# Moving the last two latent query tiles behind the first maxima of the sliding-window attention

## The reference, cut to what matters

```
h = rms_norm(x, attn_norm[l]);  proj = h @ w_in[l]        # q, k, v, u, c_q, c_kv, k_rope
out_a = swa_mixer(q, k, v, ...)    # sliding window of 128, 6 heads of 64, 2 key heads, bias, sinks
out_b = pool_mixer(u, ...)         # windowed means of 2, 4, 8, 16 tokens, then a small product
out_c = mla_mixer(c_q, c_kv, k_rope, ...)   # latent attention, 6 heads of 64 + 32 rotary
x = x + concat(out_a, out_b, out_c) @ w_out[l]
x = x + (silu(h2 @ w_gate) * (h2 @ w_up)) @ w_down
```

## Time and profile before

| | |
|---|---|
| median of 3 runs | 2482.35 us (2479.43 to 2487.03) |
| the profiled execution | 2481.47 us |
| its span in the trace | 2479.7 us |
| mean granted TensorE clock | 0.974 |
| TensorE busy | 2331.0 us (94%) |
| GpSimd busy | 1661.9 us (67%) |
| VectorE busy | 1051.8 us (42%) |
| ScalarE busy | 501.6 us (20%) |
| DMA | 207.93 MB, mean 84 GB/s |

### The profile page before, as it was taken

How to read it: one execution, slowest core, us unless ns; L and a number is a source line. 1 busy time by engine, 2 the same in 40 slices (tenths; PEclk the granted TensorE clock), 3 DMA queues, 4 the chain that set the end, 5 groups by cost and what they waited for, 6 DMA issues and landing times.

```text
span 2479.7 us, 29722 instructions
## 1 busy us (share of the span) xinstructions
PE 2331.0 (94%) x11040; PEld 1901.3 (77%) x11040; DVE 1051.8 (42%) x1342; ACT 501.6 (20%) x955; POOL 1661.9 (67%) x1370
## 2 busy tenths in 40 slices
PE   5968999999996899999999699999999898999999
PEld 4766788888876678888887468888888776888887
DVE  7664533322366344332237545215334333540430
ACT  3245211110134521111012521001111263100000
POOL 5466677767756667777777577767766564776774
PEclk9988999999998899999999899999999999999999
DMA  4300122222330012222232112222232200222222
GB/s 145 107 27 18 68 102 95 91 87 93 117 107 18 18 69 102 97 89 87 94 124 102 52 68 88 99 102 96 91 119 86 86 35 17 85 102 102 85 102 85
DMA packets 37844, 207.93 MB, mean 84 GB/s; under 512 B 3532, under 2 KB 10316, under 8 KB 16888
## 3 DMA queue, kind: packets, MB, share of 16 engines
q1 hardware_dynamic: 37752, 206.70, 23.9%
HBM read 204.55 MB, written 2.13 MB: 83 GB/s over the span
## 4 chain that ended last, share of the span: by engine, by line
PE 60%; DVE 2%; POOL 2%; ACT 2%; issue 1%; DVEq 0%; POOLq 0%; ACTq 0%
PE ps L821 18%; PE ps L826 18%; PE ps L825 18%; POOL wl L649 1%; PE ps L1185 1%; PE ps L1159 1%; ACT rt L1335 1%; POOL wh L643 0%; PE ps L1160 0%; PE ps L1163 0%; PE ps L1161 0%; DVE sq L1705 0%; DVE t L1713 0%; DVE nt L1705 0%; PE ps L1200 0%
## 5 line engine op out<-in xcount | busy, mean ns | idle before, releaser
L649 POOL TENSOR_TENSOR wl<-raw,wh 128x512 fp32r<-128x512 f32 (+1 forms) x776 | 1032.8, 1361 | 0.0
L643 POOL TENSOR_SCALAR wh<-raw 128x1024 fp32r<-128x1024 f32 (+1 forms) x388 | 427.3, 1121 | 595.3 <-PE ps L821 462.6
L821 PE MATMUL ps<-h,wh 128*128 128x512 f32 x1576 | 618.1, 392 | 18.4 <-POOL wl L649 9.2
L825 PE MATMUL ps<-h,wh 128*128 128x512 f32 x1576 | 615.2, 390 | 0.0
L826 PE MATMUL ps<-h,wl 128*128 128x512 f32 x1576 | 615.1, 390 | 0.0
L821 PE MATMUL ps<-act,wh 128*128 128x512 f32 x1120 | 437.6, 391 | 1.1 <-DVE x L1705 1.1
L825 PE MATMUL ps<-act,wh 128*128 128x512 f32 x1120 | 436.0, 389 | 0.0
L826 PE MATMUL ps<-act,wl 128*128 128x512 f32 x1120 | 436.0, 389 | 0.0
L821 PEld LDWEIGHTS ps<-h,wh 128*128 128x128 f32 x1576 | 297.0, 188 | 85.5 <-issue 24.4
L825 PEld LDWEIGHTS ps<-h,wh 128*128 128x128 f32 x1576 | 296.9, 188 | 62.3 <-issue 1.0
L826 PEld LDWEIGHTS ps<-h,wl 128*128 128x128 f32 x1576 | 297.0, 188 | 62.1
(11 more groups left out here) (337 smaller groups left out, 2681.8 us busy)
## 6 DMA issues: line engine op xcount, KB each, us to landing
raw<-w_gu SPq DMA_DIRECT2D x44, 1024.0 KB, 4.8
raw<-w_up SPq DMA_DIRECT2D x32, 1024.0 KB, 4.8
raw<-w_down_b SPq DMA_DIRECT2D x32, 1024.0 KB, 4.8
raw<-w_down_a SPq DMA_DIRECT2D x32, 704.0 KB, 4.0
raw<-w_in_a SPq DMA_DIRECT2D x14, 1024.0 KB, 4.9
raw<-w_in_f SPq DMA_DIRECT2D x13, 1024.0 KB, 4.8
raw<-w_in_r SPq DMA_DIRECT2D x11, 1024.0 KB, 4.8
raw<-w_out_a SPq DMA_DIRECT2D x8, 1024.0 KB, 7.6
```

What stands on the lines that cost most here:

```text
L643: pool.tensor_scalar(hi_s[:, part], raw[s][:, part], 1.0, 1.0, ALU.mult, ALU.mult).then_inc(hi_done, 1)
L649: ins = pool.tensor_tensor(lo_s[:, part], raw[s][:, part], hi_s[:, part].bitcast(F32), ALU.subtract)
L821: first = pe.matmul(out, w_hi, v_hi, start=start, stop=False)
L825: pe.matmul(out, w_hi, v_lo, start=False, stop=False)
```

## The change

VectorE's loop over the six query tiles is cut to four, and its body becomes a function of its own. The last two tiles are taken in `attention`, behind `maxima(0, 1)` and ahead of `head_stat`. The counts are corrected by what `bk.close` and `sqr.n += 17` have added by then. The lists of the other engines are as before, and VectorE issues the same instructions as before in another order.

```diff
-                s0 = sqr.n
                 if l == 0:
                     dve.wait_ge(st_ext, 32)
-                for i in range(MLA_HEADS):
-                    b, u = (18 + i) % 4, (18 + i) // 4
-                    dve.wait_ge(ready[b], bk.filled(b, u))
-                    dve.wait_ge(sq_ready, s0 + 12 + i)
-                    tt(qc[0:96, i, :], ps[b][0:96, :], cgq[0:96, :], ALU.mult)
-                    tt(ts[64:96, :], ps[b][96:P, :], cgq[96:P, :], ALU.mult, bk.empties(b, u))
-                    tt(qc[64:96, i, :], qc[64:96, i, :], ts[64:96, :], ALU.add)
+                for i in range(4):
+                    latent_query(i, 0)
                 sqr.n += 17
                 bk.close(late(USES_IN_A))
+
+            def latent_query(i, closed):
+                b, u = (18 + i) % 4, (18 + i) // 4
+                u -= closed and late(USES_IN_A)[b]
+                dve.wait_ge(ready[b], bk.filled(b, u))
+                dve.wait_ge(sq_ready, sqr.n + (i - 5 if closed else i + 12))
+                tt(qc[0:96, i, :], ps[b][0:96, :], cgq[0:96, :], ALU.mult)
+                tt(ts[64:96, :], ps[b][96:P, :], cgq[96:P, :], ALU.mult, bk.empties(b, u))
+                tt(qc[64:96, i, :], qc[64:96, i, :], ts[64:96, :], ALU.add)
...
                 prep(m, l, 1)
                 maxima(0, 1)
                 if m.name == "swa":
+                    for i in (4, 5):
+                        latent_query(i, 1)
 
                     head_stat(5, -1, T, 1)
```

## The result

The changed kernel takes 2486.97 us against 2481.89 us before (medians of 22 runs each, taken in turn on one chip). The ratio is 1.0015 with a 95% interval of 1.0009 to 1.0021: 0.15% slower (2.2 to 5.2 us by the interval; the two medians are 5.1 us apart), where 2.8 us of gain were forecast, and above the range's upper end of 2485.5. The profiled execution took 2487.45 us (before: 2481.47), with a span of 2485.7 us.

The account below looks back on a forecast made before the run. VectorE was taken to bound the changed stretch, with TensorE waiting. A gain of 1.57 less 0.2, so 1.4 us per layer, together 2.8, took the median 2482.35 to 2479.5 us; range 2475.0 to 2485.5.

Parts of the forecast that it names:

- Steps 1 and 2: VectorE, moved piece: maxima first, ending 5.4 us sooner; tiles 4 and 5 follow, head_stat starts as before at 755.18.
- Step 3: TensorE, column scores of head 0: start at 751.3, pause for bank 3, end some 757.0; costs about 1 of 5.4 us.
- Step 4: VectorE before maxima(1, 1): score_rows(1, 1) comes some 4 us sooner, at about 758.2, so the 2.29 us wait goes.
- Step 5: VectorE: third prep waits about 2 us for GpSimd, starts at 766.3; later wait for score_rows(2, 1) shrinks up to 1.57 us.
- the sum: Both layers: 1.57 us less 0.2 for the locks, so 1.4 us gained per layer, together 2.8 us.
- Step 6: From 768.64 on, head stages follow each other without a fixed time, so the gain carries to the span's end at full size.
- The slower one: VectorE's five all-SBUF instructions cost 8.2 us through GpSimd locks; 1.8 us later per layer, 2486.0 us; chance 0.13.
- The wait only moves: GpSimd's windows hold the second unit and banks 2 and 3 eat TensorE's lead; no gain, 2482.3 us; chance 0.16.
- the full lead: TensorE keeps its 4.5 us lead in each layer; 2473.3 us; chance 0.05.

Follow-up runs that it names:

- a3: Changed kernel with head_stat's first instruction ahead of the last two tiles, moving the statistics from bank 5 to idle bank 4; 2482.51 us, ratio 1.0003.
- a2: Changed kernel with all of head_stat put ahead of the last two query tiles; 2482.56 us, ratio 1.0001.
- b1: Kernel before with only maxima(0, 0) moved ahead of the last two tiles, prep and maxima(0, 1) staying behind them; 2481.30 us, ratio 1.0000.
- b2: Kernel before with 41 unused products in three TensorE waits ahead of the first column scores; 2480.57 us, ratio 0.9999.

## Why the prediction was wrong, point by point

- **Steps 1 and 2 held.** The maxima came first and `head_stat` started 9.25 us into the piece, forecast 9.0. VectorE bounds that piece and its length stayed.
- **Step 3 is the one that failed.** "They would start at 751.3 ... and end at some 757.0": in the same count they start at 751.4 and their 24 products end at 756.7, and bank 3 is free in time. But `score_columns(0)` has a 25th product, into bank 5, and bank 5 belongs to `head_stat`, which by step 2 does not move. It waited 2.31 and 2.74 us (2.3 to 3.3 over three profiles), and taking that wait away (a3) takes the loss away. I followed two of the three banks that the step writes.
- **Step 4** built on it. `score_rows(1, 1)` was to be done at 758.2; in the same count it was done at 761.3. VectorE's wait did go in the second layer (and fell from 2.26 to 0.85 us in the first), but only because its own `tensor_scalar` before it took 1.31 us in place of 0.31, against GpSimd. `maxima(1, 1)` gained 0.9 us in the second layer, not 2.3, and TensorE nothing: ScalarE, held for 10.5 us by `maxima(1, 0)`, had the exponentials of head 0 to make first.
- **Step 5 held in its first half**: in the second layer GpSimd released the third `prep` after 1.60 us, at 766.2 in the old count (forecast 766.3). **Its second half failed**, and it is the term that the sum was made of: VectorE's wait of 1.57 us for `score_rows(2, 1)` was to shrink by up to all of itself (1.4 us per layer in the sum). It became 4.49 us in the second layer and 1.83 (before 1.59) in the first.
- **Step 6 failed.** "Without a fixed time in them": TensorE's clock is such a thing. The lead cut its work into pieces with waits between, and in the second layer head 1's column scores went from 2.87 to 5.18 us. "At full size" could not be tested either: the time outside this place moves by more between two profiles of one kernel (2204.4 and 2200.5) than the 2.8 us that were to be carried.
- **The rivals.** The slower one came nearest in time (2486.0) for the wrong reason: the five instructions with all inputs in SBUF cost 1.22 + 1.36 + 0.33 + 1.17 + 1.31 = 5.4 us where 4.1 were paid before and 8.2 were its price. *The wait only moves* describes a2, a3 and b1. The sentence against the full lead, that a higher clock "would not help", was right for a rise (b2) and hid that a fall would hurt.
- **The Trainium skill's rule** on the lock ("SBUF — State Buffer", section "SBUF: two separate sides") agrees with this trace: the `tensor_scalar` of 762.38 ends at 763.69, and GpSimd's pair of instructions beside it (761.04, 2.62 us) at 763.66. It was worth 1.0 us here, not the sign. The floor of such a `tensor_scalar` is 0.23 us (771.82 in the kernel before, with GpSimd idle), a little below the 0.3 that the forecast used.

## What to carry to other kernels

Before an order is changed, list every bank that the step which is to run ahead will write, and who frees each; and follow its output through the next engine's list to the first instruction there that has not moved. A lead that ends in a wait is not neutral. Here it cost more than it brought, in part because the clock came down behind the waits it opened. Products added to hold the clock are not free either: if it is already low they run at the low clock and hold up the work behind them. When a small reordering moves the time by a few us, compare the stages whose code is unchanged as well, and profile the kernel before twice.

## What the runs showed of the hardware

- The 24 products of one head's column scores took 2.87 us at a granted clock of 1.00 and 5.18 us at 1.2 GHz. Behind the open wait for bank 5 (2.3 to 3.3 us) the clock fell each time (four profiles, both layers), though TensorE had work at hand again.
- Behind a wait of 1.8 to 2.7 us ahead of head 1, with the one for bank 5 filled or gone, it fell in four places of eight; with both filled or gone, in none of eight. The medians: first filled 2486.0, second filled 2489.0, both 2484.2 and 2483.4, neither 2487.0.
- Ten idle products of 512 columns took 2.56 us at the full clock and 4.25 us in a stretch where it was low at first.
- A `tensor_scalar` on 128 x 2 numbers took 0.23 us with GpSimd idle and up to 1.36 us beside GpSimd; the long ones of 1.09, 1.31 and 1.36 us ended within 0.03 us of GpSimd's instruction.
